# Compression pieces of a streamed weight sequence grouped by four instead of by two

## The reference, cut to what matters

```python
def _compress(kv, pos_emb, w1, w2):          # kv: (1, 256, 2, 128); n_c = 15 windows of 32 tokens
    blocks = kv[:, idx] + pos_emb[None, None, :, None, :]
    flat = blocks.transpose(0, 1, 3, 2, 4).reshape(B, n_c, Hkv, CMP_BLOCK * D)   # 4096 wide
    return jax.nn.silu(flat @ w1) @ w2       # w1: 4096 x 256, w2: 256 x 128

def second_block(x, w_in, ...):
    h = _rmsnorm(x, norm_g)
    proj = h @ w_in                          # 2048 x 5912: q, k, v, gates of both halves
    ...
    kc = _compress(_rope(kca), cmp_k_pos, cmp_k_w1, cmp_k_w2)
    vc = _compress(vca, cmp_v_pos, cmp_v_w1, cmp_v_w2)
    o_cmp, p_cmp = _compressed_attention(qa, kc, vc)
    ...
    return _rmsnorm(x + concat([y_a, y_b]) @ w_out, final_g)
```

## Time and profile before

| what | value |
|---|---|
| median of 3 runs | 1199.94 us |
| profiled run, whole | 1200.0 us |
| profiled run, span of the trace | 1198.2 us |
| PE busy | 1188.3 us (99%) |
| DVE, ACT, POOL busy | 753.2, 609.4, 110.8 us |
| weight loads (queue q1) | 214.59 MB |
| mean granted clock of PE | 0.998 |

### The profile page before, as it was taken

One profiled execution on the slowest core, in us unless ns is written; L12 is line 12 of the kernel. 1 busy time (PEld: TensorE's weight loads), 2 busy tenths in 40 slices (PEclk: granted clock), 3 DMA queues, 4 the chain that ended last, 5 costly groups with the idle time before them and its releaser, 6 DMA issues.

```text
span 1198.2 us, 16074 instructions
## 1 busy us (share of the span) xinstructions
PE 1188.3 (99%) x6330; PEld 992.3 (83%) x6330; DVE 753.2 (63%) x990; ACT 609.4 (51%) x895; POOL 110.8 (9%) x149
## 2 busy tenths in 40 slices
PE   9999999999999999999999999999999999999997
PEld 7899888888878888888888888888777778888886
DVE  5776977766575666556455554676665656676654
ACT  6656554644433456534434444574446446555443
POOL 0002020259700110000000000000000000000000
PEclk9999999999999999999999999999999999999999
DMA  8878776566744455555665686566556455454862
GB/s 290 259 207 249 207 198 192 165 207 182 205 135 139 143 163 149 179 187 171 207 192 188 193 293 197 184 199 221 202 187 217 158 193 176 126 156 151 297 195 96
DMA packets 145530, 229.24 MB, mean 191 GB/s; under 512 B 12658, under 2 KB 63538, under 8 KB 144432
## 3 DMA queue, kind: packets, MB, share of 16 engines
q1 hardware_dynamic: 142016, 214.59, 57.7%
q0 software_dynamic: 3120, 12.57, 3.3%
q10 hardware_dynamic: 320, 1.06, 0.2%
HBM read 220.35 MB, written 4.72 MB: 188 GB/s over the span
## 4 chain that ended last, share of the span: by engine, by line
PE 99%; DMA 0%; ACT 0%; DVE 0%; issue 0%; SPq 0%; POOLq 0%; POOL 0%; ACTq 0%
PE acc L2094 69%; PE acc L2084 10%; PE acc L2086 5%; PE aux L1973 4%; PE acc L2035 3%; PE aux L2283 1%; PE aux L2311 1%; PE acc L2425 1%; PE aux L2058 1%; PE aux L2172 1%; PE aux L2276 1%; PE aux L2304 1%; DMA raw_w<-in_w_in 0%; PE aux L2221 0%; PE aux L2213 0%; PE aux L2168 0%
## 5 line engine op out<-in xcount | busy, mean ns | idle before, releaser
L1406 DVE TENSOR_TENSOR lo_w<-raw_w,hi_w 128x1024 fp32r<-128x1024 f32 (+2 forms) x381 | 464.3, 1225 | 327.0 <-ACT hi_w L1002 325.3
L2094 PE MATMUL acc<-hi_w,h_both 128*128 128x512 f32 (+3 forms) x1800 | 559.5, 385 | 0.0
L1002 ACT ACTIVATE hi_w<-raw_w 128x1024 fp32r<-128x1024 f32 (+2 forms) x381 | 394.1, 1049 | 285.9 <-PE acc L2094 185.0
L2094 PEld LDWEIGHTS acc<-hi_w,h_both 128*128 128x128 f32 x1800 | 332.3, 188 | 67.6 <-issue 4.9
L2094 PE MATMUL acc<-lo_w,h_both 128*128 128x512 f32 (+3 forms) x900 | 341.1, 379 | 0.0
L2094 PEld LDWEIGHTS acc<-lo_w,h_both 128*128 128x128 f32 x900 | 169.4, 188 | 28.7
L2084 PE MATMUL acc<-h_both,hi_w 128*128 128x512 f32 x512 | 180.3, 397 | 0.0
L2086 PE MATMUL acc<-h_both,lo_w 128*128 128x256 f32 x512 | 142.9, 279 | 0.0
L2084 PEld LDWEIGHTS acc<-h_both,hi_w 128*128 128x128 f32 x512 | 96.1, 188 | 23.0
L2086 PEld LDWEIGHTS acc<-h_both,lo_w 128*128 128x128 f32 x512 | 96.4, 188 | 0.1
L2094 PE MATMUL acc<-hi_w,m_hi 128*128 128x512 f32 x224 | 87.7, 391 | 0.0
(11 more groups left out here) (355 smaller groups left out, 1177.8 us busy)
## 6 DMA issues: line engine op xcount, KB each, us to landing
raw_w<-in_w_in SPq DMA_DIRECT2D x275, 512.0 KB, 4.1
raw_w<-in_w_out SPq DMA_DIRECT2D x64, 512.0 KB, 4.7
raw_w<-in_w_branch_a SPq DMA_DIRECT2D x16, 512.0 KB, 4.6
raw_w<-in_w_branch_b SPq DMA_DIRECT2D x16, 512.0 KB, 4.8
raw_w<-in_cmp_k_w SPq DMA_DIRECT2D x8, 512.0 KB, 6.2
raw_w<-in_cmp_v_w SPq DMA_DIRECT2D x8, 512.0 KB, 6.2
raw_w<-in_w_in SPq DMA_DIRECT2D x8, 384.0 KB, 4.6
x_in<-in_x SPq DMA_DIRECT2D x8, 256.0 KB, 7.3
```

Of the source, the lines that this page charges most:

```text
L1002: act.activation(piece_flat(hi_w[slot], no), piece_flat(raw_w[no % RAW_SLOTS], no), ACT.Copy).then_inc(*hi_ready.event(no))
L1406: dve.tensor_tensor(piece_flat(lo_w[slot], no), piece_flat(raw_w[no % RAW_SLOTS], no), piece_flat(hi_w[slot], no).bitcast(F32), ALU.subtra ...
L2094: i = pe.matmul(to[:, t, 0:group.cols], x[at], w[:, k], start=first and k == 0 and m == 0, stop=last and k == n - 1 and m == 2)
```

## The change

```diff
-CMP_RUN, CMP_EVERY = 2, 6
+CMP_RUN, CMP_EVERY = 4, 12
```

## The result

The changed kernel takes 1213.94 us (median of four runs: 1212.27, 1212.44, 1215.44, 1215.72), the kernel before 1199.95 us beside it. The ratio is 1.0117, with a 95% interval from 1.0098 to 1.0137: slower. The forecast was 1211.0 with a range from 1205 to 1217. The profiled run took 1212.44 us, 12.4 more than the profiled run before.

The account below looks back on a forecast made before the run. PE, busy 99% of the span, bounds the kernel. Four runs lose 2.2 + 4.8 + 2.2 + 3.2 = 12.4 us, less 1.4 for merging: +11.0 on 1200.0, so 1211.0 us, range 1205 to 1217.

Parts of the forecast that it names:

- The direct wait: At the second full piece behind each run of four, PE waits 2.2 us for its split: 8.8 us.
- The queue behind the late split in the second run: Mask, exponentials and `att_p` stand behind the late split: PE waits 1.0 us at transposes, 1.9 at value products; run loses 4.8.
- The third run: Its attention step is narrow and PE finds the exponentials done, so it loses only 2.2 us.
- The fourth run: Mask chain as long, but no values copied: 2.2 us plus 1.0 at the exponentials, 3.2 us lost.
- The merging: Four runs instead of eight pairs save four fixed parts of 0.35 us on PE: a gain of 1.4 us.
- The clock: PE's clock stays at its upper level, 1.00, through waits of 2.2 us.
- Rival C: PE's clock falls in five waits, 2.77 us more each: adds 14 us, about 1225 us; chance 0.03.
- The sum: Losses of the four runs, 2.2 + 4.8 + 2.2 + 3.2 = 12.4 us, less 1.4 for merging: +11.0 us.
- A: Only the direct wait counts, since ACT and DVE catch up: +7.4 us, 1207.4 us; chance 0.20.
- B: The backlog spreads and each run loses what the second does: +17.8 us, 1217.8 us; chance 0.12.
- SP's waits for compression pieces: Sign of the forecast: four waits of SP for L2058 longer than before; no size given.

Follow-up runs that it names:

- with filler: Changed kernel plus four useless matmuls on PE ahead of the wait for the late split at the first and third run; 1211.87 us, ratio 1.0098.
- with the late split: Changed kernel with the split of the second full piece behind each run moved behind the steps of the first full tick behind the run; 1209.46 us.
- the two kernels with own buffers: Four extra raw buffers for compression pieces alone: with the changed kernel's runs of four 1198.23 us, with the kernel before's pairs 1199.69 us.
- single pieces: Kernel before with its pairs split into sixteen runs of one compression piece, behind three full pieces each; 1202.46 us, ratio 1.0024.
- runs of three: Instead of the changed kernel's runs of four, runs of 3, 3 and 2 pieces for each weight, five shared raw buffers; 1210.78 us, ratio 1.0093.
- the kernel with one such stop, at the first run: Kernel before with only the first two pairs merged into one run of four, the other six pairs kept; 1201.64 us, ratio 1.0017.

## Why the prediction was right, and where it was off

**The direct wait: right.** Predicted 2.2 us in each of four runs, at the second full piece. Measured from first matmul to first matmul, less 2.77: 854.40 - 849.44 gives 2.19 in the first, 2.14 in the second, 948.31 - 943.42 gives 2.12 in the third, 996.67 - 991.87 gives 2.03 in the fourth; 8.5 us for 8.8. ACT was released at T+4.30 to T+4.45. The chain has 3.6 to 3.7 us for the load. The estimate of 3.2 us from the Trainium skill, "DMA: Bandwidth & Descriptors", section "Anatomy of one DMA — SWDGE (gpsimd) path", was too low here too; that fit is for loads issued on another path than SP's.

**The queue behind the late split in the second run: right.** Predicted T+13.5, T+19.0 and T+20.7 for the end of the exponentials, of `att_p` and for the next full piece; measured T+13.7, T+18.8, T+20.6. The two stops were 0.8 and 1.3 us where 1.0 and 1.9 were predicted, since the time that PE takes to these places was counted too short: the run of four is 0.12 us longer, the direct wait ends at T+6.77, and the bracket leaves out the start of the first matmul. Counted from start to start against the rows of the kernel before, the two stops cost 0.9 and 1.4 us. The run lost 20.6 - 15.2 - 0.86 = 4.5 us for 4.8 (0.86 for the two more compression pieces). The kernel with that merge alone measured it: +4.2 us with the merge's gain.

**The third run: wrong.** The prediction gave it the direct wait alone, 2.2 us, because its attention step is narrow and PE would find the exponentials done. It cost 3.8 to 4.3. Two things were put at nothing: `att_p` of the wide attention step ahead of the run, which is late behind the split of the first full piece behind it (PE stops for 0.3 us in the changed kernel, 0.8 with filler, 1.0 with the late split), and the transposes of a rope step's result behind the direct wait, which wait for the mask chain (0.67 us with filler; in the changed kernel the clock had fallen there). The prediction looked at this chain only for the exponentials, and not for who else needs it done.

**The fourth run: right where the clock doesn't fall.** Its wait at the exponentials appears as 0.72 us (predicted 1.0) in the kernel with filler, and is covered by the fall where there is one.

**The merging: right.** 1.46 us for 1.4, by the two kernels with own buffers, and 2.8 us the other way by single pieces. A compression piece was put at 0.37 us and takes 0.43, which the merging leaves as it is.

**The clock: wrong.** The prediction said that the clock stays at 1.00 in waits of 2.2 us, on the strength of a silence of 2.7 us at the end of the kernel, and gave a fall 0.03; by its own words it would be wrong if the clock left 1.00. It fell behind two of the four stops in one profile and three in the other. The error was in what the row can show: at the end of the kernel PE didn't work again, and of the ten falls in these profiles nine begin after PE has resumed, by up to 1.4 us, and one just before. The Trainium skill, "TensorE: Matmul & The Clock Gate", section "Why this matters for your kernels", asks that gaps stay under about 3 us; the stops here were about 2 us and falls came all the same, so the measurement decides against it. Rival C's price was too high as well: 1.7 us for a fall instead of 2.77, and less where it covers a wait.

**The sum: 11.0 forecast, 12.4 and 14.4 in the two profiles, 14.0 at the median.** What each run of four lost can be counted from PE's rows around it, each held against the same row of the kernel before, less 0.86 us for the two more compression pieces. At the first run the scores ahead of it start at 846.93 instead of 848.80, and the transposes behind it at 859.98 instead of 858.76: 1.87 + 1.22 - 0.86 = 2.2 us. In the same way (us lost; "fall" where the clock fell):

| run | forecast | changed kernel | changed kernel, second time | with filler |
|---|---|---|---|---|
| first | 2.2 | 2.2 | 3.8 (fall) | 2.4 |
| second | 4.8 | 4.6 | 4.4 | 4.6 (fall) |
| third | 2.2 | 4.1 (fall) | 4.3 (fall) | 3.8 |
| fourth | 3.2 | 3.7 (fall) | 3.8 (fall) | 3.2 |
| sum | 12.4 | 14.6 | 16.3 | 14.0 |

Less 1.5 for the merging, and less the 0.6, 0.4 and 0.5 us by which these profiled runs were ahead of that of before already at 821 us, this gives 12.5, 14.4 and 12.0; the profiled runs are 12.4, 14.4 and 12.0 above that of before. So a fall takes 1.7 us from PE, but the kernel loses 1.6 by it only at the first run, where no other wait follows. At the second it loses nothing, at the third and the fourth 0.3 to 0.6, since the fall covers the wait that would follow. For the third and fourth this rests on one profile without a fall, that of the filler. The table's entries without a fall add up to 13.8, less 1.5: +12.3, an estimate for a run in which the clock never falls. The forecast's +11.0 is 1.3 short of it, by the third run (1.6 too little) less 0.2 for the second. The rest of the distance to the median fits the clock; no execution without a fall was profiled. That the median came within 3 us of the forecast was in part chance: two runs took 1212.3 and 1212.4 us and two 1215.4 and 1215.7, and no run stood near 1213.94.

**The rivals.** A (1207.4) is ruled out by the second run alone (+4.2) and by the runs of three, B (1217.8) by the first run, which waits once. The third and the fourth run do lie between the forecast and B.

**What would show it.** One of the signs was wrong: SP's waits for compression pieces were to be longer. They are 42.4 us in 12 where they were 65.6 in eight; the single pieces, with 124.0 us and no wait of PE, show that this number doesn't go with PE's loss at all.

**The expectation for runs of three** failed for the reason that the prediction itself named: it looked only at where PE needs the piece, and not at what stands behind its split on DVE and ACT.

## What to carry to other kernels

In a ring of buffers that two kinds of work share, count for each item how far ahead of its use its buffer comes free, and do it again when the order changes: here four places taken by short work left 4.5 us for a chain of 6.75. Then look at what stands behind the late item on every in-order engine; moving one split behind the small steps of its tick saved 10.5 us with runs of three, without making its data come earlier. A wait on the engine that bounds a kernel can cost more than its length, through the clock, and less where another wait would have come behind it; so hold whole stretches against each other, and don't add up brackets.

## What the runs showed of the hardware that wasn't expected

- Behind stops of TensorE of about 2 us the granted clock went to 0.50 (1.2 GHz) in some executions and not in others: behind two of four stops in one profile of the changed kernel, three of four in the other. Every fall was about 3.4 us long and took 1.7 us from PE. The kernel lost about 1.6 us by it where no wait followed, and 0 to 0.6 where one did. In the kernel with runs of three, three stops of 1.9 to 2.2 us had none behind them and one had. What decides it stays open.
- In the kernel with one such stop, at the first run, the times stood in two heaps 1.7 us apart (around 1201.4 and 1203.1 us).
- A run of small matmuls into 32 output partitions costs 0.35 us besides its matmuls, alike for runs of one, two and four pieces, a third of it in the first large matmul behind it.
